# Late sums one by one in a projection, inverses on four corners and shared block transfers: one change to a fused two-block kernel

## What is computed

```python
shift, scale, gate = split(silu(c) @ w_ada + b_ada, 3)
h = rmsnorm(x, norm_g) * (1 + scale) + shift
u = h @ w_in
y = concat(gdn_mixer(uc, u), rwkv_mixer(uc, u))
x = x + gate * (y @ w_out)
```

## Time and profile before

| | |
|---|---|
| three runs | 3533.51, 3535.72, 3541.87 us; median 3535.72 |
| the profiled execution | 3534.95 us, its span 3533.2 us |
| busy of the span | TensorE 84%, VectorE 57%, ScalarE 29%, GpSimd 20% |
| mean granted clock of TensorE | 0.924 of 2.4 GHz |
| late reads (L1365) | 256 of 256 KB, 3.5 us from issue to landing |
| VectorE before L2049 | 239.4 us of idle time, 235.0 of them for a late read |
| GpSimd | idle through the RWKV scan |

### The profile page before, as it was taken

How to read it: one execution, slowest core, us unless ns; L and a number is a source line. 1 busy time by engine, 2 the same in 40 slices (tenths; PEclk the granted TensorE clock), 3 DMA queues, 4 the chain that set the end, 5 groups by cost and what they waited for, 6 DMA issues and landing times. The chain is left out here.

```text
span 3533.2 us, 71437 instructions
## 1 busy us (share of the span) xinstructions
PE 2973.7 (84%) x30614; PEld 2473.7 (70%) x30614; DVE 2012.3 (57%) x3463; ACT 1012.2 (29%) x1636; POOL 708.9 (20%) x526
## 2 busy tenths in 40 slices
PE   5898888878788888388998967886979999998897
PEld 2586777666667777388888856775867877786484
DVE  5556556565554565345555556774241799997123
ACT  3243334333232222112222223322012444323102
POOL 0001111110010111000000000002864334374283
PEclk9899999988888998699999979997999999999998
DMA  9525555545555556323333224433423222221322
GB/s 388 199 76 156 154 171 166 163 152 162 171 179 175 189 180 202 118 81 94 96 86 101 74 83 145 130 115 152 155 84 125 79 83 78 84 84 60 119 95 72
DMA packets 265242, 465.90 MB, mean 132 GB/s; under 512 B 108224, under 2 KB 156576, under 8 KB 258544
## 3 DMA queue, kind: packets, MB, share of 16 engines
q1 hardware_dynamic: 213152, 364.52, 31.4%
q0 software_dynamic: 20672, 67.27, 6.5%
q10 hardware_dynamic: 31120, 29.72, 2.7%
HBM read 382.40 MB, written 81.63 MB: 131 GB/s over the span
## 5 line engine op out<-in xcount | busy, mean ns | idle before, releaser
L1365 POOL DMA_DIRECT2D arena_p<-in_w_ada x256 | 137.5, 537 | 1208.2 <-DVE arena_p L2049 624.3
L1139 PE MATMUL pjl<-high,w_high 128*128 128x512 f32 x816 | 325.4, 399 | 29.0 <-DVE low L2810 16.4
L1140 PE MATMUL pjl<-low,w_high 128*128 128x512 f32 x816 | 320.8, 393 | 0.0
L1141 PE MATMUL pjl<-high,w_low 128*128 128x512 f32 x816 | 320.6, 393 | 0.0
L2049 DVE SCALAR_TENSOR_TENSOR arena_p<-arena_p,csk 128x512 f32<-128x512 f32 x240 | 180.4, 752 | 239.4 <-DMA arena_p<-in_w_ada 235.0
L3238 DVE SCALAR_TENSOR_TENSOR arena<-arena,par 128x512 f32<-128x512 f32 x232 | 293.1, 1263 | 6.8
L1122 POOL TENSOR_TENSOR w_low<-ring_o,w_high 128x1024 fp32r<-128x1024 f32 x88 | 226.7, 2576 | 6.9
L1249 PE MATMUL xu<-h_high,wh_in 128*128 128x512 f32 x512 | 221.0, 432 | 0.0
L2880 POOL TENSOR_TENSOR w_low<-ring_o,w_high 128x1024 fp32r<-128x1024 f32 x64 | 169.3, 2646 | 250.1 <-ACT w_high L3067 249.7
L1120 POOL TENSOR_TENSOR w_high<-ring_o,cst 128x1024 fp32r<-128x1024 f32 x88 | 171.1, 1944 | 213.0 <-PE pjl L1141 67.8
L1268 DVE TENSOR_TENSOR wl_in<-ring,wh_in 128x1024 fp32r<-128x1024 f32 x136 | 165.9, 1220 | 82.8 <-ACT wh_in L1261 82.5
(11 more groups left out here) (506 smaller groups left out, 6922.4 us busy)
## 6 DMA issues: line engine op xcount, KB each, us to landing
ring<-in_w_lr SPq DMA_DIRECT2D x136, 512.0 KB, 4.5
arena_p<-in_w_ada POOLq DMA_DIRECT2D x256, 256.0 KB, 3.5
arena_p<-in_w_ada SPq DMA_DIRECT2D x32, 1024.0 KB, 8.8
ring_o<-in_w_out SPq DMA_DIRECT2D x64, 512.0 KB, 3.8
ring_o<-in_w SPq DMA_DIRECT2D x64, 512.0 KB, 3.8
arena_r<-rk_d SPq DMA_DIRECT2D x47, 384.0 KB, 4.7
rk_d<-arena_p SPq DMA_DIRECT2D x72, 192.0 KB, 2.0
arena_p<-gate_rows SPq DMA_DIRECT2D x32, 386.0 KB, 6.5
```

The source lines that it names most:

```text
L1139: pe.matmul(lat, wh[:, c], ah, start=kk == 0, stop=False)
L1140: pe.matmul(lat, wh[:, c], al, start=False, stop=False)
L1141: last = pe.matmul(lat, wl[:, c], ah, start=False, stop=kk == KT - 1)
L1365: pool.dma_start(late[:, x % 2], io["w_ada"][8 + x // 16, :, x % 16]).then_inc(S[f"p_la{x % 2}"], 16)
```

## The change

It has three parts.

1. `later(due)` does one sum, and only if fewer than `due` have been done; it is called in many more places, in `streams`, `sums`, `head` and `next_head` too, between the operations. Two `while` loops make up what is missing before L2018 and before a head's last convolution. The first 16 sums leave the norms and are spread over the later front; the late columns of the first group move from behind the front's columns to just before the first pair; TensorE waits for the bias sum in pair 0; five of the first sixteen reads are issued between transfers of gate rows. A pair's last three places are behind its L2026, for sums of the next group.
2. `products`, `turn_back`, `left` and `right` loop over the chunks alone, and issue both directions of a chunk together; d = 1 is put on the crossed corners (rows 0 to 63 with columns 64 to 127, and the reverse). One signal stands for both directions, and who copies or adds waits for all.
3. Blocks 4 to 7 of `blocks_out` are stored by GpSimd in place of ScalarE; `inverse_in` becomes eight transfers of half the size, four by SyncE for d = 0 and four by GpSimd for d = 1.

The core of the diff:

```diff
...
-            later(6)
             weights(6)
             row(6)
-            later(6)
...
             row(7)
-            later(4)
             mods(3)
...
+        reads()
         pool.wait_ge(S["b_eg"], 2)
...
+
+
+def inverse_in_crossed(eng, e, S, q, a, Z, d, back):
+
+    eng.wait_ge(S[q + "_h3"], 32 * a + 32)
+    for k in range(4):
+        g = (2 * k + 4 * d) % 8
+        eng.dma_start(Z[32 * k:32 * k + 32, d],
+                      e["zb_d"][6 * d:6 * d + 6, g:g + 2].rearrange("u g (i j) -> (g i) u j", j=16)).then_inc(back, 16)
...
-            late_reads(pool, 0, 16)
-            front_pool(pool)
+            late_reads(pool, 0, 11)
+            front_pool(pool, lambda: late_reads(pool, 11, 16))
             late_reads(pool, 16, 256)
...
+                if i == 0:
+                    pe.wait_ge(S["p_ld"], 1)
                 lora_products(0)
...
-            late_columns(pe, front_cols, 16)
...
             pe.wait_ge(S["b_gc"], 6)
+            late_columns(pe, pair_cols, 16)
...
                     link(dve.tensor_tensor_scan(cs[:, n0:n0 + 384][:, back], rst[d][:, back], sg[:, n0:n0 + 384][:, back], 0.0, ALU.mult, ALU.add))
+                later(16 * i + 32)
                 dve.tensor_tensor(sg, cs, sg, ALU.subtract).then_inc(S["p_cs"], 1)
...
                 link(dve.tensor_tensor(bb, kk, av, ALU.mult))
+                later(16 * i + 32)
...
                 dve.tensor_tensor(bb, bb, gn, ALU.mult)
+                later(16 * i + 32)
                 dve.tensor_tensor(kd, kd, gn, ALU.mult)
+                later(16 * i + 32)
                 dve.tensor_tensor(sg, kk, sg, ALU.mult)
...
+                due = 16 * h + 144
                 head_conv(h, 0)
-                if h:
-                    later(2)
+                later(due)
                 head_silu(h, 0)
                 if h:
                     weights(m + 6)
+                    later(due)
                 head_conv(h, 1)
                 if h:
-                    later(2)
+                    later(due)
                     weights(m + 7)
-                    later(2)
+                    later(due)
                 head_silu(h, 1)
+                later(due)
                 weights(m + 8)
+                while x_[0] < due:
+                    later(due)
                 head_conv(h, 2)
...
+                due = 16 * h + 160 if more else 0
...
                     weights(m + 2)
-                    later(3)
+                    later(due)
                     weights(m + 3)
-                    later(3)
+                    later(due)
...
                 link(dve.tensor_tensor(qkv[:, 1], qkv[:, 1], sqk, ALU.mult))
+                later(due)
                 dve.scalar_tensor_tensor(qkv[:, 0, 0:LAT], qkv[:, 0, 0:LAT], float(P) ** -0.5, sqq, ALU.mult, ALU.mult)
+                later(due)
...
                 for d in range(2):
                     link(dve.tensor_tensor(KB[:, d], KB[:, d], qkv[:, 1], ALU.mult))
+                    later(due)
                 for d in range(2):
                     dve.tensor_tensor(KBG[:, d], KB[:, d], EG[:, d], ALU.mult)
+                    later(due)
...
+                    later(due)
...
+                due = 16 * i + 32
+                if i == 0:
+                    late_kept(0)
                 dve.wait_ge(S["p_rt"], i * 2 + 2)
                 link(dve.reciprocal(nr, nr))
                 link(dve.scalar_tensor_tensor(kk, k, prm(i, R_KK), nr, ALU.mult, ALU.mult))
+                later(due)
                 sums(i, 0)
-                later(2)
+                later(due)
                 weights(m + 2)
-                later(1)
+                later(due)
                 weights(m + 3)
-                later(2)
+                later(due)
                 streams(i, 0)
-                later(1)
+                later(due)
                 if i == PAIRS - 1:
                     dve.wait_ge(S["p_lo"], 2 * PAIRS)
                     dve.memset(raw[:], 0.0).then_inc(S["q_v0"], 1)
                 weights(m + 4)
-                later(2)
+                later(due)
                 weights(m + 5)
-                later(2)
+                later(due)
                 sums(i, 1)
-                later(3)
+                later(due)
                 weights(m + 6)
-                later(3)
+                later(due)
                 streams(i, 1)
+                while x_[0] < due:
+                    later(due)
                 dve.wait_ge(S["p_x"], i * 2 + 2)
                 dve.scalar_tensor_tensor(kds, r, prm(i, R_RK), kds, ALU.mult, ALU.mult).then_inc(S["p_rk"], 1)
                 weights(m + 7)
                 dve.tensor_tensor(kds, v[:, 0:LAT], up[0][:, 0:LAT], ALU.mult).then_inc(S["p_bv"], 1)
                 dve.wait_ge(S["p_bv"], 1 + i + 1)
                 if i < PAIRS - 1:
+                    later(due + 1)
                     mixes(i + 1, 2, "p_mv")
+                    later(due + 2)
                     weights(m + 9)
+                    later(due + 3)
                 else:
...
-            def later(n):
-
-                for x in range(x_[0], min(x_[0] + n, 256)):
+            def later(due):
+
+                x = x_[0]
+                if x < due:
...
-                x_[0] += n
+                    x_[0] += 1
...
             lora_mix(0)
-            late_kept(0)
+            later(16)
             weights(10)
...
+    TILES4 = [(d, hs, HEADS[h ^ d]) for d in range(2) for h, hs in enumerate(HEADS)]
...
+            for a in range(2 * PAIRS):
+                pool.wait_ge(S["r_pa"], a * 2 + 2)
+                blocks_out(pool, e, LT[a % 2], range(4, 8), S["r_g1"])
+                inverse_in_crossed(pool, e, S, "r", a, Z, 1, S["r_g4"])
...
-                inverse_in(sp, e, S, "r", a, Z)
+                inverse_in_crossed(sp, e, S, "r", a, Z, 0, S["r_h4"])
...
-                for d in range(2):
-                    pe.wait_ge(S["r_tt"], a * NT + (l - 1) * 2 + d + 1)
-                    for u in range(UN):
-                        last = [pe.matmul(o[hs, d, u], LT[a % 2][hs, d, u], T[hs, d, u], start=True, stop=True) for hs in HEADS]
-                    done(last, "r_x")
+                pe.wait_ge(S["r_tt"], a * NT + (l - 1) * 2 + 2)
+                for u in range(UN):
+                    last = [pe.matmul(o[hs, d, u], LT[a % 2][to, d, u], T[to, d, u], start=True, stop=True) for d, hs, to in TILES4]
+                done(last, "r_x")
...
-                    act.wait_ge(S["r_p"], a * 8 + 2 * d if a else 2 * d + 2)
+                    act.wait_ge(S["r_p"], a * 8 + 2 if a else 4)
                     act.activation(LT[a % 2][:, d], o[:, d], ACT.Copy).then_inc(S["r_pa"], 1)
-                act.wait_ge(S["r_pa"], a * 2 + 2)
-                blocks_out(act, e, S, "r", a, LT[a % 2], range(4, 8))
...
                 dve.wait_ge(S["r_h4"], 64 * a + 64)
+                dve.wait_ge(S["r_g4"], 64 * a + 64)
                 dve.tensor_tensor(TT[a % 2][:].rearrange("p d u (b j) -> p (d u) b j", j=16),
```

More of the change, by code:

```diff
@@ L408, in front_scalar, with front_vector @@
         return columns, logits, exponential, decays
-    def front_vector(dve, weights, link, later):
+    def front_vector(dve, weights, link):
         def normed(k0, k1):
@@ L570, in front_vector, with front_pool @@
         return columns, softplus, cumulated, products_of, kept
-    def front_pool(pool):
+    def front_pool(pool, reads):
         pool.wait_ge(S["b_scan"], 2)
@@ L2061, in late_kept @@
                     dve.tensor_tensor(mod2[:, k], cols, pr("b_ada2", 48)[:, k], ALU.add).then_inc(S["p_ld"], 1)
-            columns, softplus, cumulated, products_of, kept = front_vector(dve, weights, link, later)
+            columns, softplus, cumulated, products_of, kept = front_vector(dve, weights, link)
             def tables():
@@ L2099, in _ @@
             lora_mix(2)
+            later(16)
             lora_mix(3)
+            later(16)
             weights(12)
+            later(16)
             cumulated(0)
+            later(16)
             weights(13)
+            later(16)
             mixes(0, 0, None)
+            later(16)
             weights(14)
+            later(16)
             cumulated(1)
+            later(16)
             weights(15)
+            later(16)
             mixes(0, 1, "p_kr")
+            later(16)
             weights(16)
+            later(16)
             mixes(0, 2, "p_mv")
+            later(16)
             products_of()
             weights(17)
+            later(16)
             kept()
+            later(16)
+            assert x_[0] == 16
             for i in range(PAIRS):
@@ L2280, in products @@
                 pe.wait_ge(S[("r_la", "r_lc")[a % 2]], a // 2 * 48 + 48)
-                for d in range(2):
-                    for u in range(UN):
-                        last = [pe.matmul(o[hs, d, u], BX[a % 2][hs, d, u], KA[a % 2][hs, d, u], start=True, stop=True) for hs in HEADS]
-                    done(last, "r_p")
+                for u in range(UN):
```

(33 more changed lines are left out.)

37 lines of the change are left out of this document (19 added, 18 removed).

## The result

The changed kernel took 3400.18 us in the median of four runs (3394.76 to 3407.23), the kernel before 3538.8 on the same chip. The ratio of the runs is 0.96, with an interval from 0.9558 to 0.9641: faster, by 139 us. The profiled execution has a span of 3397.9 us for 3533.2; TensorE is busy 86% of it for 84%, VectorE 59% for 57%, GpSimd 23% for 20%.

The account below looks back on a forecast made before the run. Neither TensorE nor VectorE was full; VectorE's waits for late reads and the chain of pairs and heads were taken to bound the kernel. -70 - 37 - 7 - 3 = -117 gave 3418 us; own range 3398 to 3442, full range 3345 to 3480.

Parts of the forecast that it names:

- Pairs: Projection's eight pairs: moving the late sums saves 9.3 us in six, 6.5 in the first, 8.0 in the last: -70.
- B: Stretch of a pair from second scan to L2018, 20.7 us: loses waits and four sums, -9.0, to 11.7.
- C: Stretch of a pair from L2018 to the next reciprocal, 19.4 us: half of full clock's gain, near -1.3.
- A: Stretch of a pair from reciprocal to second scan, 39.7 us: paced by the read slots, +1.0.
- T: Time from the end of a late-read slot's sum to its next sum's possible start; taken as 3.7 us.
- Heads: Projection's seven heads: fewer sums and waits on the chain to TensorE's L1556, -5.3 each, -37 in all.
- Front: Front before the pairs: sixteen sums leave the space between weight pieces and norms: -7, between -9 and +5.
- RWKV: RWKV scan: merged matmuls -2, ScalarE's spared issues -5, back transfer +4: -3, from -10 to +19.
- Rival 1: RWKV matmuls: four corners run side by side, 90 us of pitch, some 60% on the path: -54 more, 3364; chance 0.21.
- Transfers: RWKV block transfers: back transfer +0.3 us in each of 13 halves, +4; ScalarE's four fewer issues a half, -5.
- Rival 4: Pairs: TensorE or weights set the chain, so sums move idle time only: within 0.3% of 3536; chance 0.05.
- the slower rival: Eight sums before a pair's or head's first stores, T beyond 6.3: slower; at T = 8 +76.5, 3611; chance 0.03.

Follow-up runs that it names:

- late_only: The kernel before with the late sums of the change alone, its RWKV scan and block transfers left old: 3410.14 us, ratio 0.9629.
- rwkv_only: The kernel before with the RWKV part of the change alone (four corners in one loop, shared transfers): 3527.56 us, ratio 0.998.
- transfers_only: The kernel before with the shared block transfers alone, uncrossed, its matmuls in two loops on two corners: 3542.95 us, ratio 1.001.
- one_slot: The changed kernel with one slot for the late reads in place of two: 3735.96 us, ratio 1.0531.
- idle_sums: The changed kernel with two sums a pair and three of a head's five convolution sums moved into VectorE's idle time: 3413.93 us, ratio 0.9639.

## Why the prediction was right, and where it was off

The forecast was 3418 us, from a sum of -117; it was 3400, and the range held it. By its steps:

- **Pairs, -70 forecast, -89 in the trace.** B lost 8.55 us in the mean (in all but the first 8.9; forecast 9.0), C 1.4 (forecast 1.3). Both terms were of the right size, and the half of full clock that the forecast took for C is the mean of pairs that got all of it, some or none. A was to grow by 1.0 and shrank by 1.0: this is the term that was mis-sized, 2 us a pair, 16 in all. Its new value was right, 13.65 + 3T = 24.75 at T = 3.7, and 24.6 in the trace (23.91 and the last operation's 0.69). Its base was not: the earlier trace rows are of one pair whose first streams end at 23.7, and the mean of the pairs before is 25.3. Another 0.4 came from the time of the stores, with three sums in it instead of five.
- **Heads, -37 forecast, -32.** The part behind the second convolution was exact: from 1153.17 to 1155.63 in one head, 2.46 us for 2.5. The stores of a head come back 13.3 us after its last preparation for 12.8, which the sum did not have.
- **Front, -7 forecast, -11.** ScalarE's longest wait there for the norms' scales (L354, for L433) fell from 37.1 to 25.0 us, which is more than the two waits of the earlier trace rows together, 9.1; the sum had taken off 1.9 for the late columns.
- **RWKV, -3 forecast, -7 in the trace, and 0.2% with an interval that holds zero when run alone.** That the size was right was luck, since the reason was wrong. The prediction held that four corners would not shorten the pitch; they halve it, 15.6 ns for 29.2. Rival 1 was right in its mechanism, and the Trainium skill's TensorEngine Tiling (Array Packing), Key Properties, with it: tiles on different corners load and multiply side by side, and the trace agrees with 15.6 ns. The floor of about 25 ns from start to start, which the prediction took from the Trainium skill's page TensorE: Matmul & The Clock Gate, does not hold in these rows, where four corners take turns. Rival 1 then failed at its price: of 90 us of pitch it put 54 on the path by a guessed share of 60%, and the stretch lost 7 us, with TensorE 50 us less busy. Nearly all of it was off the path. Only the first turn and the products lie in the ring, 1.3 us a half at best (twice the 1.40 - 0.75 of the rows above). The last link, 0.6 to 0.8 us longer, took half of that; whether copies that wait for both directions and the lower clock took the rest is not shown.
- **Transfers, +4 - 5 forecast.** The last link grew by 0.6 to 0.8 us a half (forecast 0.3, bound 1.6). ScalarE's four issues gave what the forecast said, but not in time: TensorE's waits for that copy, 5.4 us before and 4.3 in late_only, are gone in after, rwkv_only and transfers_only, and they stay (7.5 and 7.9) in the two kernels that leave the issues to ScalarE. The half did not become shorter for it, 34.79 us in transfers_only. So the -5 of the sum were no cost on the path.
- **Rival 4** and the slower rival did not happen; the condition of the latter, T beyond 6.3, never held for long. Its price was undersized, as one_slot showed.

## What to carry to other kernels

Filler work that waits for its own transfers is not free where the engine's program is in order: put each piece where the engine would idle, one at a time, and only as many as their transfers can feed in that time, or the last of them stands in front of the work that the idle time was waiting for. Leave the time of the important stores thin, since reads and stores lengthen each other there. Before an engine is made quicker in a stage, follow the stage once around its ring: here TensorE lost 50 us of work for 7 us of time, because a half waits for six links of which it has a small part in one. Where a link is shortened and the time stays, look for what has moved into its place in the next link, as the store behind the loads did.

## What the runs showed of the hardware

- Records of 64 x 64 float32 matmuls on all four corners start 15.6 ns apart, on the two straight corners 29.2 ns, in one loop or two. Per corner that is one in 62 and in 58 ns. So what the earlier trace rows showed as a price of the record was one of the corner.
- The way back of the inverses, from first issue to use, took 4.8 us as four transfers on SyncE, 8.4 as eight halves on SyncE, 5.4 to 5.6 as four halves each on SyncE and GpSimd.
- A small store right behind three loads of 384 KB on one queue landed after 4.4 us in the median of the scan, with the loads 5 us ahead after 2.2, and with them on another queue but 1.7 us ahead after 3.9.
- A late read that a sum waited for turned its slot around in 3.4 us in the median in front of the stores of streams, and in 4.4 during them (6.6 at most, idle_sums). With two, three and five reads issued during those stores, ScalarE was released 9.9, 11.7 and 12.1 to 12.6 us after the streams.
- The same stretch of a pair (C) took 16.8 us at a granted clock of 1.00, 18.5 at 0.91 and 20.1 at 0.83.
